# Ring transfers of 1 MB, each sent when its own megabyte has been read, in place of 2 MB slots

## The reference

```
x = x + concat[RMSNorm(attention), RMSNorm(s5)] @ W_out
logits = xn2 @ w_router + b_router;  top_v, top_i = top_k(logits, 4);  gates = softmax(top_v)
for each expert e of 32, for the tokens that chose it:
    h   = xn2 @ w_gate_up[e] + b_gate_up[e]              # 1024 -> 2048
    g   = min(h[..., ::2], 7);  l = clip(h[..., 1::2], -7, 7)
    out = (g * sigmoid(1.702 * g) * (l + 1)) @ w_down[e] + b_down[e]   # 1024 -> 1024
    x  += gate * out
```

## Time and profile before

| | |
|---|---|
| median of 3 runs | 1100.65 us |
| profiled execution | 1100.01 us |
| its span, first to last instruction | 1098.2 us |
| TensorE busy | 980.6 us (89%) |
| VectorE, ScalarE busy | 390.8 us (36%), 207.5 us (19%) |
| DMA queue of SP | 423.56 MB, 92.3% of 16 DMA engines' span |
| ring transfers of 2 MB | 120 of `gu_ring`, 63 of `dn_ring` |
| mean granted clock | 0.982 |

### The profile page before, as it was taken

One profiled execution on the slowest core, in us unless ns is written; L12 is line 12 of the kernel. 1 busy time (PEld: TensorE's weight loads), 2 busy tenths in 40 slices (PEclk: granted clock), 3 DMA queues, 4 the chain that ended last, 5 costly groups with the idle time before them and its releaser, 6 DMA issues.

```text
span 1098.2 us, 16660 instructions
## 1 busy us (share of the span) xinstructions
PE 980.6 (89%) x6622; PEld 416.4 (38%) x6622; DVE 390.8 (36%) x893; ACT 207.5 (19%) x451; POOL 9.6 (1%) x10
## 2 busy tenths in 40 slices
PE   9989999999997999799988999799779879869976
PEld 7777773332332333233323333233223323323322
DVE  8996565222322132213232322123333323222222
ACT  7784441110110011111101110011011111101111
POOL 2010000000000000000000000000000000000000
PEclk9989999999999999999999999899999999999999
DMA  9515947999999999999999999999999999999995
GB/s 370 139 50 191 403 202 306 408 420 428 409 426 426 428 416 427 426 428 419 427 427 427 428 423 427 428 428 429 425 427 428 426 426 428 428 427 428 428 420 233
DMA packets 43228, 425.22 MB, mean 387 GB/s; under 512 B 11412, under 2 KB 14740, under 8 KB 16656
## 3 DMA queue, kind: packets, MB, share of 16 engines
q1 hardware_dynamic: 42720, 423.56, 92.3%
q10 hardware_dynamic: 432, 0.52, 0.1%
HBM read 419.86 MB, written 2.51 MB: 385 GB/s over the span
## 4 chain that ended last, share of the span: by engine, by line
PE 61%; DMA 26%; DVE 6%; ACT 4%; issue 3%; DVEq 0%; SPq 0%; POOL 0%; ACTq 0%; POOLq 0%
PE banks L548 58%; DMA gu_ring<-w_gu_dram 26%; PE banks L998 1%; DVE raw L2025 1%; ACT s_p L1333 1%; PE banks L949 1%; ACT x_tok L1435 1%; PE banks L1075 1%; DVE hl L2037 1%; DVE hT L2042 1%; ACT s_p L1345 1%; PE banks L1005 0%; ACT gath L1446 0%; DVE s_p L1809 0%; ACT pT L1357 0%
## 5 line engine op out<-in xcount | busy, mean ns | idle before, releaser
L548 PE MATMUL banks<-gu_ring,xe 128*64 128x512 f32 x1152 | 269.6, 606 | 14.2 <-DMA gu_ring<-w_gu_dram 14.2
L2071 DVE TENSOR_TENSOR xT<-xT,banks 128x576 f32<-128x576 f32 x128 | 91.0, 751 | 534.1 <-PE banks L548 534.1
L548 PE MATMUL banks<-gu_ring,xe_s 128*32 128x512 f32 x1152 | 153.4, 624 | 48.9 <-DMA gu_ring<-w_gu_dram 30.8
L548 PEld LDWEIGHTS banks<-gu_ring,xe 128*64 128x64 f32 x1152 | 76.1, 138 | 169.3 <-issue 143.2
L548 PE MATMUL banks<-dn_ring,hT 128*64 128x512 f32 x576 | 129.3, 597 | 4.9 <-DVE hT L2042 4.9
L548 PEld LDWEIGHTS banks<-gu_ring,xe_s 128*32 128x32 f32 x1152 | 29.1, 110 | 137.5 <-issue 95.0
L548 PE MATMUL banks<-dn_ring,hT_s 128*32 128x256 f32 x1152 | 67.8, 381 | 3.3 <-ACT xe_s L1480 3.2
L548 PEld LDWEIGHTS banks<-dn_ring,hT 128*64 128x64 f32 x576 | 39.2, 137 | 79.4 <-issue 73.0
L1461 ACT ACTIVATE raw<-banks 128x512 f32<-128x512 f32 x18 | 10.8, 598 | 233.2 <-PE banks L548 233.2
L548 PE MATMUL banks<-x_tok,oh 96*64 96x512 f32 (+1 forms) x228 | 51.0, 578 | 0.5 <-DVE oh L1996 0.3
L548 PEld LDWEIGHTS banks<-dn_ring,hT_s 128*32 128x32 f32 x1152 | 34.9, 110 | 36.2 <-issue 15.1
(11 more groups left out here) (359 smaller groups left out, 850.7 us busy)
## 6 DMA issues: line engine op xcount, KB each, us to landing
gu_ring<-w_gu_dram SPq DMA_DIRECT2D x120, 2048.0 KB, 23.4
dn_ring<-w_dn_dram SPq DMA_DIRECT2D x63, 2048.0 KB, 21.2
gu_ring<-w_gu_dram SPq DMA_DIRECT2D x16, 1024.0 KB, 8.3
w_out<-w_out_dram SPq DMA_DIRECT2D x2, 2048.0 KB, 13.0
w_in<-w_in_dram SPq DMA_DIRECT2D x3, 1024.0 KB, 12.1
w_in<-w_in_dram SPq DMA_DIRECT2D x4, 512.0 KB, 8.2
w_glu<-w_glu_dram SPq DMA_DIRECT2D x1, 2048.0 KB, 8.9
dn_ring<-w_dn_dram SPq DMA_DIRECT2D x2, 1024.0 KB, 23.1
```

Of the source, the lines that this page charges most:

```text
L548: return nc.tensor.matmul(out, lhsT, rhs, start=start, stop=stop, **kw)
L2071: X.tensor_tensor(two, two, pair[(1, 3)[n % 2]].rearrange("p (h f) -> p h f", h=2)[:, :, 0:T], ALU.add).then_inc(S("acc_done"), 1)
```

## The change

Every ring transfer is now 1 MB. `load_gu` takes a row `r` and fills one half of a slot; SP waits for one count of `gu_used` before each. `load_dn` takes a chunk `c` and fills one half of a slot after one count of `dn_used`. Two transfers now raise the semaphore of one slot, so TensorE waits for 32 where it waited for 16; it still waits once for each slot, for both halves. For each partition a transfer now moves 8 KB instead of 16 KB; in HBM the pieces of one transfer lie 16 KB apart.

```diff
-    def load_gu(sp, x, k):
+    def load_gu(sp, x, r):
+        k, i = r // GU_ROWS, r % GU_ROWS
...
-        sp.dma_start(gu_ring[k][:], src).then_inc(gu_in[k], 16)
-
-    def load_dn(sp, x, h, j):
+        sp.dma_start(gu_ring[k][:, i], src[:, i]).then_inc(gu_in[k], 16)
+
+    def load_dn(sp, x, c, j, signal=None):
+        h, rows = c // 2, slice(2 * (c % 2), 2 * (c % 2) + 2)
...
-        sp.dma_start(dn_ring[2 * j + h][:], src).then_inc(dn_in[2 * j + h], 16)
+        sp.dma_start(dn_ring[2 * j + h][:, rows], src[:, rows]).then_inc(signal or dn_in[2 * j + h], 16)
...
     def gu_filled(p, k):
 
-        if isinstance(p, int) and p < 2:
-            return 16 * GU_ROWS * (p + 1)
-        return p * 16 + 16 * (2 * GU_ROWS - 1)
+        return p * (16 * GU_ROWS) + 16 * GU_ROWS
+
+    def dn_filled(fill):
+
+        return fill * 32
...
         def gu(x, p_before):
-            for k in range(GU_SLOTS):
-                sp.wait_ge(S("gu_used"), p_before * 8 + GU_ROWS * (k + 1))
-                load_gu(sp, x, k)
+            for r in range(KT):
+                sp.wait_ge(S("gu_used"), p_before * 8 + (r + 1))
+                load_gu(sp, x, r)
 
         def dn(x, p_before, j):
-            for h in range(2):
-                sp.wait_ge(S("dn_used"), p_before * 4 + 2 * (h + 1))
-                load_dn(sp, x, h, j)
+            for c in range(4):
+                sp.wait_ge(S("dn_used"), p_before * 4 + (c + 1))
+                load_dn(sp, x, c, j)
...
-                    pe.wait_ge(dn_in[2 * j + c // 2], fill * 16)
+                    pe.wait_ge(dn_in[2 * j + c // 2], dn_filled(fill) - (16 if after is None and c == 2 else 0))
```

More of the change, by code:

```diff
@@ L365, in first_dn @@
     def first_dn(sp, j):
-        for h in range(2):
-            sp.dma_start(dn_ring[2 * j + h][:], dn_rows(j, h)).then_inc(dn_in[2 * j + h], 16)
+        for c in range(4):
+            h, rows = c // 2, slice(2 * (c % 2), 2 * (c % 2) + 2)
+            sp.dma_start(dn_ring[2 * j + h][:, rows], dn_rows(j, h)[:, rows]).then_inc(dn_in[2 * j + h], 16)
     def load_others(sp):
@@ L401, in load_others @@
         gu(x[1], NE - 2)
[L402 to L408, removed]
+        for c in range(4):
+            sp.wait_ge(S("dn_used"), (NE - 3) * 4 + (c + 1))
+            load_dn(sp, x[1], c, 1, S("dn_last") if c == 3 else None)
     LAST_PARTS = ((0, 3, False), (2, 1, True), (1, 2, True), (3, 0, True))
@@ L529, in _ @@
                 x = sp.snap(x_reg, min_val=0, max_val=NE - 1)
[L530 to L536, removed]
+                for r in range(KT):
+                    sp.wait_ge(S("gu_used"), j * 8 + (8 * (NE - 1) + (r + 1)))
+                    load_gu(sp, x, r)
+                for c in range(4):
+                    sp.wait_ge(S("dn_used"), j * 4 + (4 * (NE - 1) + (c + 1)))
+                    load_dn(sp, x, c, 0)
         for k, c in enumerate((0, 2, 1, 3)):
```

## The result

The changed kernel took 1110.85 us as the median of 4 runs (1110.27 to 1112.56), the kernel before 1100.78 us beside it: a ratio of 1.0098, 95% interval 1.008 to 1.0115, 10.1 us slower. The profiled execution took 1112.56 us, 1.9 us of it outside its span of 1110.7 us. Forecast were 1110 us.

The account below looks back on a forecast made before the run. The prediction took the DMA stream to bound the kernel from about 200 to 1078.9 us. 1100.01 us + 12.5 for smaller pieces - 1.8 - 1.0 at dry places gave 1109.7, about 1110 us; 8-in-10 range 1102 to 1115 us.

Parts of the forecast that it names:

- The bound: From about 200 to 1078.9 us the DMA stream sets the time; 19.3 us of fixed work follow.
- The cost: From 191 to 1062.9 us, 178 old 2 MB transfers each take 0.07 us more: 12.5 us.
- The lower measure: At 177 to 190 us, 425 GB/s against 428 at 650 to 780 us: 0.035 us per transfer, 6.2 us.
- rival (a): In the stream, pieces cost only what the GB/s show, 0.035 us: about 1104 us; chance 0.15 for 1102 to 1105.
- The gains: Earlier issue regains time where the DMA queue is dry: 2.8 us together, between 0 and 4.3.
- The 1.0 us for 281 us: At 281 to 285 us, a landing 7.0 us after the last instead of 4.9; finer issue regains 1.0 us.
- the one at 401 us: Dry place at 401 us; with that at 520 us, 0.4 us lost on the mean engine, no gain taken.
- The sum: Profiled 1100.01 us + 12.5 - 1.8 - 1.0 = 1109.7 us; about 1110 us for the median.
- the first dry place: At 190 to 194 us, DMA share 0.44 while SP waits for expert 0's first `w_down` slot; gain 1.8 us.
- (b): 8 KB pieces keep the pace of 16 KB and earlier issue fills four dry places: 1095.7 us; chance 0.04.
- (c): The cost in the stream is hidden and the dry places don't count: 1099 to 1101 us; chance 0.05.
- (d): Part of the fixed cost returns at each transfer, or the pace costs 0.12 us: 1116 us and more; chance 0.06.

Follow-up runs that it names:

- e10: The kernel before, without the 32-token matmuls of five of eight `w_gate_up` rows in the four experts of the kind "many": 1099.05 us, 0.9988.
- e12: The changed kernel, without the 32-token matmuls of five of eight `w_gate_up` rows in the four experts of the kind "many": 1110.70 us, 1.0096.
- e8: The kernel before, with only the loop's first `w_down` in 1 MB transfers, each sent after one count: 1099.53 us, 1.0006.
- e3: The kernel before with its 2 MB transfers and waits, weights laid out in HBM so that pieces are 8 KB: 1111.37 us, 1.0104.
- e5: The kernel before with 1 MB transfers in 16 KB pieces, to even and odd partitions, sent in pairs at the old moments: 1100.27 us, 1.0007.
- e1: The changed kernel with its 1 MB transfers sent two at a time, at the moments of the kernel before: 1111.86 us, 1.0109.
- e2: The kernel before with 1 MB transfers in 16 KB pieces, each to 64 neighbouring partitions, at the old moments: 1736.87 us, median of six.
- e9: The kernel before with its 2 MB transfers and waits, weights laid out in HBM so that pieces are 4 KB: 1138.65 us, 1.0356.
- e6: The kernel before with `w_gate_up` in 4 MB transfers of 32 KB pieces, each sent after four rows: 1110.01 us, 1.0111.

## Why the prediction was right

- **The bound.** A DMA stream at a fixed pace, with TensorE beside it: shown by e10 (14 us less of TensorE's work, about 1 us) and e12 (nothing). It was not the whole truth for the first rounds of the kernel before, as e8 shows: there the two are so close that an issue 1.3 us earlier at 190 us is lost again by 281 us.
- **The cost.** I took 0.07 us for each of 178 transfers, 12.5 us. Measured are 0.06 by the last four slots and 0.07 by the GB/s of 130 and of 400 us: 10.7 to 12.5 us, and the longer ruler has the 12.5. e3 and e5 show that it is the size of the piece. I had not separated pieces from transfers; the sum needed it only because the 1 MB transfers of before had both.
- **The lower measure.** The 425 GB/s of 177 to 190 us, rival (a), was misleading: the same form gives 422 in a stretch of 130 us. Thirteen microseconds are five megabytes, and whole packets at the stretch's two ends weigh a percent. The landings, six transfers apart, were the better ruler: 6.29 MB in 14.95 us are 421 GB/s.
- **The gains.** At 190 us I forecast 1.8 us. SP sends 1.7 us earlier, and 1.2 us of it are left once the first two slots have gone. The 1.0 us for 281 us came for another reason than the one I gave: the slower stream closes that place by itself (e1), and the one at 401 us, for which I had taken nothing. That the sum of the gains fits is in part luck.
- **The sum.** Medians: + 10.1 us against + 9.7 forecast. The profiled pair can be set side by side by bytes, from the packets' records: how much later the changed kernel has moved the same number of MB on SP's queue.

  | MB moved | changed kernel later by, us |
  |---|---|
  | 40, before the first dry place | 1.3 |
  | 44, after it | 0.1 |
  | 75 and 80, around the place at 281 us | 1.1 and -0.1 |
  | 125 and 130, around the place at 401 us | 1.7 and 1.1 |
  | 200 | 3.3 |
  | 400 | 10.7 |
  | 415, near the last `gu_ring` landing | 11.4 |

  The three dry places give back 1.2, 1.2 and 0.5 us, 2.9 in all against 2.8 forecast. The rest is the pace: 11.4 - 1.3 + 2.9 = 13.0 us against 12.5 forecast. The 1.3 us from before the loop are no part of the forecast. The last landing itself moved by more, 1091.18 - 1078.90 = 12.3 us: single landings in both traces jump by 1.5 us now and then, and the profiled execution was the slowest of its four. One reading in the prediction was off without bearing on the sum: by the earlier trace rows the last megabyte of `w_down` lands at 1088.7 us, 9.8 us after the last wait and not some 8.
- **Rivals.** (b) and (c) need equal paces, refuted by 422 against 428. (d), a fixed cost returning with each transfer, is refuted by e5; its other half, a pace 0.12 us slower, by the 0.07 measured.

The Trainium skill's page "DMA: Bandwidth & Descriptors" has, in "Measured", the advice of at least 1 MiB for each transfer; e5 shows no loss from 2 MB to 1 MB in a full queue, so here it is silent about the cost that mattered. (The fit with 2.0 us, which the prediction takes from the same page, stands in its section "Anatomy of one DMA — SWDGE (gpsimd) path", for DMAs issued from GpSimd; these are SP's.) Its "Why small descriptors are slow" has the right kind of cost, a fixed one for each packet, with about 3 cycles, an estimate of 3.5 ns if they are cycles of the 850 MHz that the page gives for the fabric; measured are about 9 ns. The measurement decides: about 0.07 us for 2 MB in 8 KB pieces, not 0.03.

## What to carry to other kernels

Where DMA engines are occupied all the time, count the contiguous pieces on each engine, not the transfers: halving the pieces from 16 to 8 KB cost 1.4% of the stream here, and no finer timing could pay for it behind a queue of 20 us. Finer issue is worth something only where the queue is dry, and only if the engine that frees the buffers isn't what made it dry; check the next dry place before counting the gain at the first. Take a stream's pace from landings many transfers apart or from a long stretch. Before reading one dry place in one trace as the work of an edit, compare the granted clock of the stretch before it.

## What the runs showed of the hardware

- A stream of DMAs that each fill 64 neighbouring partitions ran at half rate, 213 GB/s at a share of 1.00 (e2; 244 later, from 650 to 780 us); with every second partition it ran at 427 (e5).
- Each further piece on an engine costs the full stream about 9 ns, from 16 to 8 KB (421 against 427 GB/s) and from 16 to 4 KB (409, e9). The number of transfers doesn't show (e5, 427).
- A piece of 32 KB goes as one packet, and the stream with it reaches 435 GB/s in a slice (e6).
- With 4 KB pieces SP can't send ahead at will. A `gu_ring` issue takes 0.33 us in the kernel before, and in e9:

```profile
L337 SPq DMA_DIRECT2D gu_ring<-w_gu_dram x120: 372/4669/9938, 200.3 to 1102.0; - x120
```

The columns are min, median and max in ns: a median of 4.7 us, about the time of one transfer, as if each issue waited until an earlier transfer's place in the queue was free (no run tests this). SPq has 10% of the chain there. With 8 KB pieces in 2 MB transfers (e3) every `gu_ring` issue took 0.37 us.
